# Where an expert's rows lie in its half: partitions in steps of eight by a table of ranks

## The reference

```
g_idx = jnp.argmax(g_logits, axis=-1)                # one of 8 groups for each token
e_prob = jax.nn.softmax(e_logits, axis=-1)           # the 8 experts of that group
top_p, top_i = lax.top_k(e_prob, TOP_K)              # TOP_K = 2
expert_id = (g_idx[:, None] * EXPERTS_PER_GROUP + top_i).reshape(-1)
order = jnp.argsort(expert_id); tok = order // TOP_K
xs = ht[tok]                                         # 2048 rows, ordered by expert
gate = lax.ragged_dot(xs, w_gate, group_sizes)       # 64 experts, 1024 -> 256
up = lax.ragged_dot(xs, w_up, group_sizes)
y = lax.ragged_dot((jax.nn.silu(gate) * up).astype(xs.dtype), w_down, group_sizes)
out = jnp.zeros_like(ht).at[tok].add(y * weights[order][:, None])
```

## Time and profile before

| | us |
|---|---|
| median of 3 runs | 2888.84 |
| lowest and highest | 2887.57, 2892.43 |
| the profiled execution | 2890.57 |
| its span from first to last instruction | 2888.8 |
| granted TensorE clock, mean over the span | 0.974 |

### The profile page before, as it was taken

How to read it: one execution, slowest core, us unless ns; L and a number is a source line. 1 busy time by engine, 2 the same in 40 slices (tenths; PEclk the granted TensorE clock), 3 DMA queues, 4 the chain that set the end, 5 groups by cost and what they waited for, 6 DMA issues and landing times. The chain is left out here.

```text
span 2888.8 us, 43048 instructions
## 1 busy us (share of the span) xinstructions
PE 2692.7 (93%) x16932; PEld 2092.5 (72%) x16932; DVE 1532.0 (53%) x2426; ACT 904.6 (31%) x1863; POOL 499.0 (17%) x579
## 2 busy tenths in 40 slices
PE   7998988999999999999999999999999789888886
PEld 5876755788778888888887887888887655555543
DVE  5647478766765887657666645554443621111113
ACT  3235168333202455543334432430030211111111
POOL 1013300000001333310300062431020211111112
PEclk9999999999999999999999999999999889999998
DMA  4121120333642355597754230002203699999996
GB/s 144 56 81 34 44 81 34 99 109 104 203 164 90 128 181 170 162 349 246 248 200 108 44 45 1 2 2 73 59 5 124 246 376 420 420 419 416 411 393 277
DMA packets 186618, 488.86 MB, mean 169 GB/s; under 512 B 20520, under 2 KB 66728, under 8 KB 160816
## 3 DMA queue, kind: packets, MB, share of 16 engines
q1 hardware_dynamic: 175328, 467.58, 45.4%
q0 software_dynamic: 10512, 16.80, 1.6%
q10 hardware_dynamic: 576, 1.70, 0.2%
HBM read 420.55 MB, written 86.05 MB: 175 GB/s over the span
## 5 line engine op out<-in xcount | busy, mean ns | idle before, releaser
L502 PE MATMUL banks<-split_weights,hT_upper 128*128 128x512 f32 x1504 | 469.7, 394 | 7.8 <-DVE hT_lower L138 4.4
L502 PEld LDWEIGHTS banks<-split_weights,hT_upper 128*128 128x128 f32 x1504 | 282.4, 189 | 68.4 <-issue 6.6
L502 PE MATMUL banks<-split_weights,hT_lower 128*128 128x512 f32 x752 | 295.2, 393 | 0.0
L4241 DVE COPY ex_y<-banks 128x512 f32<-128x512 f32 x36 | 24.9, 692 | 417.2 <-PE banks L4158 417.2
L519 PE MATMUL banks<-hT_upper,split_weights 128*128 128x512 f32 x688 | 216.7, 393 | 6.1 <-DVE split_weights L138 4.4
L2330 PE MATMUL banks<-uT_lower 128*128 128x512 f32 x912 | 210.8, 389 | 0.7 <-DVE hT_spare L2073 0.7
L4129 PE MATMUL banks<-expert_inner,ex_xT 128*64 128x256 f32 (+1 forms) x1056 | 176.5, 396 | 25.2 <-DMA expert_inner<-in_w_up 10.8
L2330 PEld LDWEIGHTS banks<-uT_lower 128*128 128x128 f32 x912 | 170.9, 188 | 36.4 <-DVE hT_spare L2073 1.1
L2002 PE MATMUL banks<-hT_upper,split_weights 128*128 128x512 f32 x576 | 188.9, 389 | 0.0
L502 PEld LDWEIGHTS banks<-split_weights,hT_lower 128*128 128x128 f32 x752 | 142.1, 189 | 30.4
L138 DVE TENSOR_TENSOR split_weights<-raw_weights,split_weights 128x512 fp32r<-128x512 f32 (+1 forms) x112 | 158.4, 1415 | 3.7 <-ACT split_weights L2022 2.3
(11 more groups left out here) (616 smaller groups left out, 5577.7 us busy)
## 6 DMA issues: line engine op xcount, KB each, us to landing
expert_inner<-in_w_gate SPq DMA_DIRECT2D x33, 1024.0 KB, 18.4
expert_inner<-in_w_up SPq DMA_DIRECT2D x33, 1024.0 KB, 29.8
expert_inner<-in_w_down SPq DMA_DIRECT2D x32, 1024.0 KB, 28.3
raw_weights<-in_w_in SPq DMA_DIRECT2D x28, 1024.0 KB, 6.8
hT<-in_w_down SPq DMA_DIRECT2D x44, 512.0 KB, 5.2
u_sums<-ff_scratch SPq DMA_DIRECT2D x16, 1024.0 KB, 5.5
hT_spare<-u_sums SPq DMA_DIRECT2D x32, 512.0 KB, 4.6
raw_weights<-in_w_up SPq DMA_DIRECT2D x28, 512.0 KB, 4.9
```

Of the source, the lines that this page charges most:

```text
L502: last = pe.matmul(bank, acts[x][:, r * KT // 2 + k, m * P:(m + 1) * P].bitcast(F32R), w[y][:, k, :].bitcast(F32R), start=(r == 0 and k == ...
L4241: nc.vector.tensor_copy(y[:, q, BANK:D], c.bank(5)).then_inc(y_dve, 1)
```

## The change

A new constant of 128 x 128 numbers, `k_rank_at`, the same in every partition, takes the place of `iota` in the comparison that makes `ohr`. Column p holds p div 64 x 64 + (p mod 8) x 8 + (p mod 64) div 8: the row number whose token comes to lie on partition p. Row number 0 of a half stays on its partition 0, row number 1 goes to partition 8, 2 to 16, 7 to 56, 8 to 1, 9 to 9, and so on. In a unit with one expert this holds in each of both halves. Gather and scatter use the same table of indices, so both move. SP loads the constant ahead of the experts' weights into a new tile `rank_at` of 64 KB, and DVE waits for it once, ahead of the one-hots.

```
+        rank_at = t("rank_at", P)
...
+        rank_there = c.sem(mem, "ro_rank_at_there")
...
         @block.sync
         def _(sp):
+            sp.dma_start(rank_at[:, :], c.io["k_rank_at"]).then_inc(rank_there, 16)
             for i in range(SOON):
                 experts.load_gate_up(sp, i, i)
                 experts.load_down(sp, i, i)
...
+            dve.wait_ge(rank_there, 16)
             for g in range(4):
...
-                v.tensor_tensor(ohr[:, g % 2, :, :].bitcast(F32R), c.k["iota"][:, 0:P].unsqueeze(1).to_broadcast([P, 4, P]),
+                v.tensor_tensor(ohr[:, g % 2, :, :].bitcast(F32R), rank_at[:, :].unsqueeze(1).to_broadcast([P, 4, P]),
                                 wide_of(rowf, P), ALU.is_equal).then_inc(onehots, 1)
...
+    k["k_rank_at"] = np.tile((i // ROWS * ROWS + i % 8 * 8 + i % ROWS // 8).astype(np.float32), (P, 1))
```

## The result

The changed kernel takes 2907.02 us (median of 4 runs, 2904.32 to 2908.68), the kernel before 2888.20 in the same comparison (4 runs, 2885.10 to 2892.43). The ratio is 1.0071, with a 95% interval of 1.0056 to 1.0085: slower by 18.8 us by the medians, by 16 to 25 us by the interval. The forecast was 2900 us, slower by 11. The sign, the stage and the mechanism came as forecast, but the loss was 1.7 times the forecast one. The profiled execution took 2904.32 us; its experts began 4.8 us earlier than before's by chance, so that its span shows 13.7 us and the stage itself more.

The account below looks back on a forecast made before the run. The prediction took the most loaded DMA engine as the bound: +10.8 us for rows, -0.3 for the last scatter, +0.5 for clocks and PE waits, together +11 on 2888.84, so 2900 us, range 2890 to 2908.

Parts of the forecast that it names:

- What bounds the kernel: Experts' stage: the most loaded of the 16 DMA engines binds, while PE waits for loads.
- the rival that the extra work is hidden: Experts' stage: PE sets the pace and the extra rows cost nothing; 2889 us, chance 0.12.
- Which engine takes which partition: Gathers and scatters: each engine serves two blocks of four partitions, the second taken to be 32 partitions on.
- The rivals with eights: Gathers and scatters: an engine serves eight neighbouring partitions; -34 us, 2855 us, chance 0.02.
- another pairing: Second blocks of engines paired otherwise: -12.3 us, 2876.5 us, or mirrored, -2.6 us; chance 0.08 for both.
- The closed sum for before: Heaviest engine's loads, rows and small packets in the earlier kernel's experts' stage: end at 2832.6 against 2834.3 us measured.
- Table, wait and one-hots at nothing: Before and early in the experts: the added table load, DVE's wait and the one-hots reading rank_at cost 0.
- 74 rows at 0.146 us: Experts' stage: 37 more rows each direction on the heaviest engine, each replacing an empty place; +10.8 us.
- the one on the gathers: Experts' gathers: 8 rows on an engine land up to 1.9 us later, hidden since used two units later; 0.
- The check on unit 0: First gather in the profile after: 4 engines with 7 rows, about 107 GB/s for 1.1 us, not 7 engines.
- More than the sum: Experts' stage: four engines behind and a row nearer 0.24 us; +17 us, 2906, more with late gathers; chance 0.10.
- The two GB/s forecasts: Unit-0 gather at about 107 GB/s; experts' stage with fewer GB/s, under 400 from 2,600 us on.

Follow-up runs that it names:

- e3_one: Changed kernel with a table that loads one engine of each half as the change does and the others evenly; 2903.61 us, ratio 1.0054.
- e8_spread: Changed kernel with the table of e4_round, and an expert with a unit of its own begun at row 32 of it; 2870.31 us, ratio 0.9949.
- e4_round: Changed kernel with a table in which consecutive ranks take turns over the eight engines of a half; 2878.12 us, ratio 0.9972.
- e2_fill: Changed kernel with a table in which ranks fill one engine's eight places after another; 2915.96 us, ratio 1.0100.
- e1_identity: Changed kernel with the table holding what iota holds, so rows lie as before; load and wait stay; 2886.24 us, ratio 1.0003.
- e9_unit0: Changed kernel with only unit 0's gather in the changed layout, by a fixed table, all else laid as before; 2889.43 us, ratio 1.0015.
- e11_always: Changed kernel, fixed table: gathers from unit 3 on fill all eight places of the first engine, opening and scatters as before; 2897.79 us, ratio 1.0044.
- e12_again: The changed kernel measured once more, unaltered; 2904.03 us, ratio 1.0060.
- e7_other: e3_one with the loaded engine moved to that of partitions 24 to 27 and 56 to 59; 2907.07 us, ratio 1.0073.
- e10_later: Changed kernel with all gathers but unit 0's in the changed layout, by a fixed table, scatters as before; 2891.65 us, ratio 1.0017.
- e6_scatter: Changed kernel with only the scatters in the changed layout, by a fixed table, gathers as before; 2893.36 us, ratio 1.0024.

## Why the prediction was half right

**What bounds the kernel.** Right. The most loaded DMA engine sets the stage, and e3_one shows it alone at work. PE's pace doesn't bound it, not even with 284 rows (e8_spread). So the rival that the extra work is hidden fell.

**Which engine takes which partition.** Right in both parts: blocks of four from the earlier trace rows, and the second block 32 on, which was only assumed and which e4_round and e2_fill bear out. The rivals with eights and with another pairing fell: by the prediction's own sum eights would have gained 34 us, and the changed kernel lost 18.8. The closed sum for before takes 170 small packets where the 70 transfers up to the last load have 560 places on this engine and 404 rows in them, so 156; that is 0.1 us.

**Table, wait and one-hots at nothing.** Right as far as e1_identity can tell. The timelines agree: the one-hots still take 0.68 us each, and the table's load took SP 0.33 us.

```profile
2282.59 0.33 SPq L3812 DMA_DIRECT2D ro_rank_at<-in_k_rank_at  x1
2282.97 0.42 SPq L3735 DMA_DIRECT2D hT<-in_w_gate  x1
...
2311.91 0.68 DVE L3970 TENSOR_TENSOR ro_ohr<-ro_rank_at,ro_rowf 128x512 fp32r<-128x512 f32 x1
```

**74 rows at 0.146 us.** Nearly right. It is 78 rows, because the scatters add 41, and the runs without a changed opening give 0.15 to 0.16 us a row (11.5 / 78, 5.4 / 34, 6.7 / 41). The term is 12 us and was 10.8.

**The step that failed** is the one on the gathers: "A gather with 8 rows instead of 4 on one engine alternates with 8 KB weight packets (0.31 us): up to 4 x 0.46 = 1.9 us later", and so hidden. It put at nothing what e9_unit0 measured at 3.2 us. That was argued for the loaded queue and for the one who waits for the gather. Nothing was said of the first gather, which meets empty queues, and of the loads behind it: 3 us on the engines that bind. The row that held the hint was used, but for another thing. The earlier trace rows gave 0.24 us a row with the first latencies; the prediction spread this price over all 74 rows as an upper bound and then dropped it. It is the price of a lone gather, and e11_always shows that later rows cost 0.15. Nor does it give the 3 us: three rows more on an engine would be 0.7. The check on unit 0 that the prediction listed (four engines with 7 rows, 1.1 us) should have been followed by the question what lands behind them.

**What that leaves.** Of the 18.8 us, 12.1 are rows (forecast 10.8), 3 are the opening (forecast 0), and 3.7 are open. e12_again, the same kernel, has only 15.8, so part of the 3.7 is spread of the whole program; but the stage by itself repeats within about 1 us (0.6 for the changed kernel, 1.2 for before's layout) and in the changed kernel lies 2.3 to 3 above the two terms. So the sum seems to lack a third term as well, and its cause stays open.

**The rest.** "More than the sum" (+17, chance 0.10) came nearest, and by its size it would have done. Of its two reasons, four late engines instead of one are not shown to matter (e3_one 17.1, changed kernel 15.8 and 18.8), and a row isn't dearer in general. "If gathers come late" points at the right place: one gather lands 0.8 us later, and the loads behind it 3. "The 54 us after it stay" was right, as were the share of 0.25 at the end, the last w_down that lands later (13.9 us later here, with a stage that began 4.8 earlier) and the landings of 30 us and more:

```profile
expert_inner<-in_w_down SPq DMA_DIRECT2D x1, 1024.0 KB, 30.4
```

"Up to 2,323 us all as before within 1 us" was not: the experts' first load is issued at 2318.96 against 2323.77, and in profiled executions of kernels that are alike up to there it stands anywhere between 2314.89 (e1_identity) and 2323.77. The two GB/s forecasts were right in kind, but the rate is already 390 at 2,500, where the forecast had the fall below 400 from 2,600 on.

**The range** ended at 2908 and holds the time by 1 us, which is luck: its upper end was drawn from the wrong price for the right rival.

## What to carry to other kernels

Where a stage is bound by DMA and the transfers are uneven over partitions, count the bytes of each of the 16 engines, by the partitions that each serves, and take the largest; a gather or scatter with empty places is such a transfer, and a table of ranks that costs nothing measurable can level it (with a lone expert's rows begun in the middle of its unit, e8_spread: 0.9949). A share of the DMA engines near 1 with falling GB/s is the sign that they aren't level, and the last microseconds of the stage show in sixteenths how many are behind. Price the first uneven transfer into empty queues by itself, with the landings of the loads behind it: on an engine that keeps its backlog to the end, what it loses at the start is lost (e9_unit0: 3.2 us).

## What the runs showed of the hardware

The 3 us at the opening were not expected. The GB/s in 40 slices by start of packets show the first gather and then the first load: kernel before over 2 us (2323.1 to 2325.1, 0.05 us a slice) and changed kernel over 2.4 us (2318.3 to 2320.7, 0.06 us a slice):

```profile
GB/s 0 2 167 165 0 0 82 0 82 246 0 164 164 0 164 246 164 164 82 246 0 82 83 0 0 1 0 0 0 0 0 0 0 819 492 164 0 0 0 0
```

```profile
GB/s 2 3 206 68 0 0 0 0 0 0 0 0 0 0 0 0 0 137 68 68 205 68 0 205 68 205 68 137 341 205 68 410 887 0 0 137 0 0 0 0
```

Before, two empty slices, 0.1 us, follow the first four rows (167 and 165 are two rows each), and then rows start steadily. In the changed kernel thirteen empty slices, 0.8 us, follow the first four (206 is three rows, 68 one). This stop is not what delays the loads. e12_again, the same kernel in another execution (2321.81 to 2324.21), has no such stop, nor has e3_one (2322.22 to 2324.62), in which all eight engines of the half have rows: no more than five slices in a row, 0.3 us, are empty there. Their first loads land after 7.2 and 7.5 us all the same:

```profile
GB/s 2 71 138 68 0 137 0 0 68 0 0 0 0 68 0 137 68 68 68 137 68 68 137 137 68 68 68 205 410 0 341 137 273 0 0 0 410 0 137 137
```

```profile
GB/s 1 71 274 137 0 0 0 0 0 205 0 410 68 68 274 0 1 1 68 0 68 0 0 68 0 68 0 410 751 0 0 68 0 137 273 0 137 0 0 546
```

What the late kernels share, by the start and length of every packet in the traces, is that the gather's rows are not done when the load begins. In all fifteen traces the first packets of the load start 0.97 to 1.06 us after its issue. With at most 4 rows on an engine the last row of the gather has ended 0.57 to 0.76 us after that issue: the all but empty slices between 83 and 819 above. With 7 or 8 rows on one engine it ends after 1.14 to 1.64 us, within the load. One engine with 7 rows is enough (e3_one). Why the loads then lose 3 us and not 1, the runs don't show. In all kernels whose first gather had 7 or 8 rows on an engine the first load landed after 7.2 to 7.9 us (for e7_other the trace has no landing of it), in all with 4 or fewer after 4.8 or 4.9.

Two engines were loaded alone, those of partitions 0 to 3 with 32 to 35 and of 24 to 27 with 56 to 59: +17.1 and +20.4 us, with intervals that overlap (e3_one, e7_other). Gathered or scattered, a row costs the same within the measurement (0.16 us each in e10_later and e6_scatter).
